# Second block: where the gates, the branch outputs and the token products lie in PSUM and in program order

## The chip, the cores and the metric

One core of one Trainium2 chip runs the whole program. The metric is the device time of one execution in microseconds. Its engines run side by side, each through its own queue in program order: TensorE (PE; its weight loads are listed as PEld), VectorE (DVE), ScalarE (ACT), GpSimd (POOL), and SyncE (SP), which issues the transfers.

## The reference, cut to what matters

Two transformer blocks follow one another on 256 tokens of width 1024. The change lies in the mixing half of the second:

```
z_a, q, k, v, gate_logits = split(h @ w_in)
u, v_ = split(gelu(z_a))
y_a = u * (tril(w_s) @ rms_norm(v_) + b_s)        # "token mixing", 768 wide
q, k = rope(q), rope(k)
y_b = dilated_mixture_attention(q, k, v)           # 256 wide
gates = sigmoid(gate_logits)                       # 2 x 1024 wide
merged = gates[0] * (y_a @ w_branch_a) + gates[1] * (y_b @ w_branch_b)
x = x + merged @ w_out
```

## The kernel before

Every weight matrix is cut into units of 128 x 1024 numbers, loaded in pairs through SyncE's queue. A unit is split into a high part `whi` (an ACT copy to the rounded type) and a low part `wlo` (a DVE subtraction), five units ahead of its use (`split_to(u + LA)` in `unit`). Activations are held in the same way, high and low: `xb` holds the normed input, transposed, as [feature, k, high|low, token], `xa` the output of the branches. A product is high x high + high x low + low x high. It is made in one of two forms:

- `mm3` (L223): three matmuls per k, each with its own weight load.
- `feature_unit` (L372): one matmul of 512 columns with `whi` against high and low joined, which lands in the two halves of a bank, and one of 256 columns with `wlo` into the first half. `join` (L382) then adds the halves: an ACT copy of the second, a DVE addition of the first. That addition frees the bank (`bank_free`).

Each engine's instructions are recorded in the order in which the Python code calls them, and each engine executes them in that order, stopping at the first whose semaphores aren't there. There is no planner: the order written by hand is the schedule. A `later(...)` function is run inside the next call of `unit`.

The order in the second block: `group_2` makes queries (groups 0 and 1, `qtok`), keys (2, 3, `ktok`), values (4, 5), and the second half of z_a (6, 7); a group of 512 columns has four units, one of 256 two. `rotate` applies the rotary embedding on POOL, `qk_transposes` (L1203) transposes two tiles of heads on TensorE and evicts them. After group 2's third unit (n == 2) stand two query transposes of two tiles each, after its fourth (n == 3) the third. Attention runs in four steps of `dl_scores`, `dl_probs` and `dl_out` between the units.

Then six `u_unit(c)` (banks c % 3) make u. `token_mix(i)` (L1307) is the product with w_s, 12, 8 and 12 matmul instructions for i = 0, 1, 2, in bank 4 + i; `token_gate(i)` (L1322) evicts it: two DVE operations into `yy`, a Gelu of u on ACT (`uT`), a DVE multiplication, an ACT copy and a DVE subtraction into `xa`. The last lines before the merge are L1378 to L1394.

The merge handles eight tiles d of 128 features. `merge_gate(d)` runs two feature units (gate of branch 0 and 1), joins them into `sg` and, in the next unit, applies the sigmoid (`squash`). `merge(d)` makes both branch outputs in bank 3, k 0 to 5 in columns 0:256, k 6 and 7 in columns 256:512, multiplies them with the gates (`mt`), adds the halves (`mx`) and splits the sum (`mh`, `ml`). The order of `merge_steps` is gate 0, gate 1, gate 2, branch 0, gate 3, branch 1, gate 4, and so on; from branch 4 on an output unit follows each branch unit, and four come at the end.

Of the kernel before, what the change touches and what calls it, by code (L numbers as in the profile page):

```python
# [7 lines left out]
ALU = mybir.AluOpType  # L8
# [6 lines left out]
KT = D // 128  # L15
# [143 lines left out]
def two_block_program(nc, T, out):  # L159
# [4 lines left out]
    def at(off, name, shape, dt=F32):  # L164
        return nc.alloc_sbuf_tensor_at(name, shape, dt, offset=off)
# [28 lines left out]
    xa = M("xa", [128, KT, 2, 256], F32R)  # L194
    xa_h, xa_l = xa[:, :, 0, :], xa[:, :, 1, :]
# [14 lines left out]
    pb = [nc.alloc_psum_tensor(f"bank{i}", [128, 512], F32) for i in range(8)]  # L210

    def semaphore(name):
        return nc.alloc_semaphore(f"s_{name}")

    sraw = [semaphore(f"raw{i}") for i in range(NR)]
    P, A, V, G = [Queue(semaphore(n)) for n in ("pe", "act", "dve", "pool")]
# [3 lines left out]
    def mm(o, l, r, start, stop, *w, inc=False):  # L220
        return P(lambda e: e.matmul(o, l, r, start=start, stop=stop), *w, inc=inc)  # L221

    def mm3(o, lh, ll, rh, rl, first, last, *w):  # L223

        mm(o, lh, rh, first, False, *w)
        mm(o, lh, rl, False, False)
        mm(o, ll, rh, False, last)

    def tr(o, i):
        P(lambda e: e.transpose(o, i, ident[:, :]), id_tok, inc=False)  # L230
# [4 lines left out]
    def copy(o, i, *w, **kw):  # L235
        return act(o, i, ACT.Copy, *w, **kw)

    def vcopy(o, i, *w):
        return V(lambda e: e.tensor_copy(o, i), *w)

    def tt(q, o, a, b, op, *w):
        return q(lambda e: e.tensor_tensor(out=o, in0=a, in1=b, op=op), *w)  # L242
# [32 lines left out]
    def flat(ap):  # L275
        return ap.rearrange("p a b -> p (a b)")
# [57 lines left out]
    def next_units(n):  # L334
        weights["unit"] += n
        return list(range(weights["unit"] - n, weights["unit"]))
# [3 lines left out]
    def later(fn):  # L340

        pending.append(fn)
# [17 lines left out]
    bank_free = {i: [] for i in range(8)}  # L360
# [11 lines left out]
    def feature_unit(u, bank, x, ready):  # L372

        h, l = unit(u)
        for k in range(KT):
            mm(pb[bank][:, :], h[:, k * 128:k * 128 + 128], flat(x[:, k, :, :]), k == 0, False,
               *(bank_free[bank] if k == 0 else []), *ready(k))
        for k in range(KT):
            mm(pb[bank][:, 0:256], l[:, k * 128:k * 128 + 128], x[:, k, 0, :], False, k == KT - 1)
        return release(u)  # L380

    def join(o, bank, p, *w):  # L382

        a = copy(o, pb[bank][:, 256:512], p, *w)
        v = tt(V, o, pb[bank][:, 0:256], o, ALU.add, a)
        bank_free[bank] = [v]
        return v
# [530 lines left out]
    def mix_1(k):  # L918
        return us[k], xb_h[:, k, :], xb_l[:, k, :], [ytok[k]]

    for k in range(KT - HOLD):
        u, lh, ll, w = mix_1(k)
        out_unit(u, (0, 1), lh, ll, k == 0, False, *w)
        release(u)
        if k == 0:
            ch_finish_0()
            P.wait(cv["out"], *bank_free[1])
            for t in range(2):
                for ft in range(2):
                    c = t * 256 + ft * 128  # L930
# [208 lines left out]
    qtok = at(xa_at, "qtok", [128, 2, 768])  # L1139
    ktok = at(xa_at + 6144, "ktok", [128, 2, 768])  # L1140
    N = Arena(C.lo)
    qt = N("qt", [128, 6, 256])
# [4 lines left out]
    sg = [K(f"sg{i}", [128, 512]) for i in range(4)]  # L1147
    mt = K("mt", [128, 512])
# [18 lines left out]
    def group_2(i, dst, c0, func=ACT.Copy):  # L1167

        w = GROUPS_2[i][1]
        banks = (2 * i % 3, (2 * i + 1) % 3)  # L1170
        us = next_units(w // 128)
        if i == 0:
            for n, u in enumerate(us):
                if n == 3:
                    norm_transposes(1, xb_h, xb_l)
                token_unit(u, (0,), xb_h, xb_l, banks, ready_x)
        for u in us:
            token_unit(u, (1,) if i == 0 else (0, 1), xb_h, xb_l, banks, ready_x)
            p = release(u)
            if u == us[-1]:  # L1180
                done[i] = []
                for t in range(2):
                    a = act(dst[:, t, c0:c0 + w], pb[banks[t]][:, 0:w], func, p)
                    bank_free[banks[t]] = [a]
                    done[i].append(a)
            yield

    def rotate(x, toks):

        r = []  # L1190
        for t in range(2):
            x3 = by64(x[:, t, :])
            x1, x2 = x3[:, :, 0:8], x3[:, :, 8:16]
            cos, sin = [rope[:, t, j, :].unsqueeze(1).broadcast_to([128, 12, 8]) for j in range(2)]
            m = [rtmp[:, j, :].rearrange("p (h d) -> p h d", d=8) for j in range(4)]
            for j, (a, b) in enumerate(((x1, cos), (x2, sin), (x1, sin), (x2, cos))):
                g = tt(G, m[j], a, b, ALU.mult, *toks, *rope_tok, *r)
            tt(G, x1, m[0], m[1], ALU.subtract, g)
            g = tt(G, x2, m[2], m[3], ALU.add)
            r = [g]  # L1200
        return r

    def qk_transposes(src, dst, b, bank, toks, scale):  # L1203
        P.wait(*toks, *bank_free[bank])
        for i in range(2):
            for t in range(2):
                tr(pb[bank][:, i * 256 + t * 128:i * 256 + t * 128 + 128], src[:, t, (b + i) * 128:(b + i) * 128 + 128])
        p = P.mark()
        if scale is not None:
            r = copy(flat(dst[:, b:b + 2, :]), pb[bank][:, :], p, scale=scale)  # L1210
        else:
            r = vcopy(flat(dst[:, b:b + 2, :]), pb[bank][:, :], p)
        bank_free[bank] = [r]
        return r
# [72 lines left out]
    def dl_finish():  # L1287
        o, src = xa_h[:, 6:8, :], pb[3][:, :].rearrange("p (k t) -> p k t", k=2)
        a = copy(o, src, *dl["out", 3])
        branch_tok.append(low(xa_l[:, 6:8, :], src, o, a))  # L1290
        bank_free[3] = [branch_tok[-1]]

    branch_tok = []
# [13 lines left out]
    def token_mix(i, toks):  # L1307

        bank = 4 + i
        P.wait(ws_tok, *toks, *bank_free[bank])  # L1310
        for c in (2 * i, 2 * i + 1):
            for t in range(2):
                o = (c % 2) * 256 + t * 128
                ga, gb = c * 128 // 192, (c * 128 + 64) // 192
                if ga == gb:
                    mm(pb[bank][:, o:o + 128], zv[:, t, c * 128:c * 128 + 128], ws[:, ga, :], True, True)
                else:
                    mm(pb[bank][0:64, o:o + 128], zv[:, t, c * 128:c * 128 + 64], ws[:, ga, :], True, True)
                    mm(pb[bank][64:128, o:o + 128], zv[:, t, c * 128 + 64:c * 128 + 128], ws[:, gb, :], True, True)
        mixed_tok[i] = P.mark()  # L1320
# [20 lines left out]
    def u_unit(c):  # L1341
        p = feature_unit(next_units(1)[0], c % 3, xb, lambda k: ready_x(k, 0) + ready_x(k, 1))
        u_tok[c // 2] = join(uT[:, c, :], c % 3, p, *junk_tok)
# [3 lines left out]
            pass  # L1347
    qr = rotate(qtok, done[0] + done[1])
    for n, _ in enumerate(group_2(2, ktok, 0)):
        if n == 2:  # L1350
            qT_tok = [qk_transposes(qtok, qt, 0, 4, qr, -0.125), qk_transposes(qtok, qt, 2, 5, qr, -0.125)]
        elif n == 3:
            qT_tok.append(qk_transposes(qtok, qt, 4, 6, qr, -0.125))
    for _ in group_2(3, ktok, 512):
        pass
    kr = rotate(ktok, done[2] + done[3])
# [20 lines left out]
    vn = v_norm()  # L1377
# [3 lines left out]
    u_unit(1)  # L1381
    u_unit(2)
    dl_probs(3)
    token_mix(0, vn)
    u_unit(3)
    dl_out(3)
    dl_finish()
    token_mix(1, vn)
    token_gate(0)
    u_unit(4)  # L1390
    token_mix(2, vn)
    u_unit(5)
    token_gate(1)
    token_gate(2)  # L1394
# [3 lines left out]
    sg_tok, m_tok, sum_tok = {}, {}, {}  # L1398

    def merge_gate(d):  # L1400
        for b, u in enumerate(next_units(2)):
            bank = (2 * d + b) % 3
            p = feature_unit(u, bank, xb, lambda k: [])
            v = join(sg[d % 4][:, 256 * b:256 * b + 256], bank, p, *sum_tok.get(d - 4, []))
        later(lambda: squash(d, v))
# [2 lines left out]
        sg_tok[d] = act(sg[d % 4][:, :], sg[d % 4][:, :], ACT.Sigmoid, v)  # L1408

    def merge(d):  # L1410
        bank, u = 3, next_units(1)[0]
        h, l = unit(u)
        P.wait(*branch_tok, *bank_free[bank])
        for k in range(KT):
            c = 0 if k < 6 else 256
            mm3(pb[bank][:, c:c + 256], h[:, k * 128:k * 128 + 128], l[:, k * 128:k * 128 + 128],
                xa_h[:, k, :], xa_l[:, k, :], k in (0, 6), k in (5, 7))
        p = release(u)
        v = tt(V, mt[:, :], pb[bank][:, :], sg[d % 4][:, :], ALU.mult, p, sg_tok[d])
        bank_free[bank] = [v]  # L1420
        x, h, l = mx[d % 2], mh[d % 6][:, :], ml[d % 6][:, :]
        v = tt(V, x[:, :], mt[:, 0:256], mt[:, 256:512], ALU.add, v)
        sum_tok[d] = [v]
        a = copy(h, x[:, :], v, *out_done.get(d - 6, []))
        m_tok[d] = low(l, x[:, :], h, a)

    out_done = {}
    for what, d in merge_steps():
# [4 lines left out]
        else:  # L1433
            u = next_units(1)[0]
# [10 lines left out]
    for t in range(2):  # L1445
        for hf in range(2):
            c = slice(hf * 512, hf * 512 + 512)
# [86 lines left out]
```

How the kernel before makes its waits and increments, by code:

```python
    def play(self, eng):  # L147
        for op in self.ops:
            if op[0] is None:
                eng.wait_ge(op[1], op[2])
            elif op[1] is True:
                op[0](eng).then_inc(self.sem, 1)
            elif op[1] is False:
                op[0](eng)
            else:
                op[0](eng).then_inc(op[1], 16)
```

## Time and profile before

| | |
|---|---|
| time, median of 3 | 699.97 us (699.76 to 700.63) |
| the profiled execution's own time | 699.81 us |
| its span, first to last instruction | 697.8 us |
| mean granted clock | 0.998 of full |
| PE busy / PE weight loads busy | 688.4 us (99%) / 593.5 us (85%) |
| DVE / ACT / POOL busy | 480.0 us (69%) / 405.5 us (58%) / 93.0 us (13%) |
| chain that ended last | PE 91%, POOL 2%, DVE 2%, ACT 2%, DMA 1% |

Shares of busy time are over the span; matmuls are pipelined, and a busy one contains its modelled drain, so a run of matmuls is to be read by the distance between starts. The gates, merges and output units of the second block lie between 415 and 499 us.

### The profile page before, as it was taken

Reading aid. Unit: us, or ns where it says so; the run is one execution under the profiler, and the core shown is the slowest. Engines: PE = TensorE matmul, PEld = TensorE weight load, DVE = VectorE, ACT = ScalarE, POOL = GpSimd, SP = SyncE. Lnnn points to the kernel's source line nnn. Section 1 sums busy time; section 2 is a strip of 40 time slices with the busy share of each in tenths; the row PEclk is TensorE's granted clock in tenths of the full one; section 3 lists DMA queues with packets and bytes.
Section 4 is the critical chain, followed back from the end, with each engine's and each line's share of the span. In section 5 each row is a group of like instructions: output and inputs, shape, how many; then the busy total and the mean of one; then the engine's idle time right before and its main releaser. Section 6 shows DMA issues by size and latency. Waiting matters only on the chain.

```text
span 697.8 us, 9554 instructions
## 1 busy us (share of the span) xinstructions
PE 688.4 (99%) x3880; PEld 593.5 (85%) x3880; DVE 480.0 (69%) x713; ACT 405.5 (58%) x678; POOL 93.0 (13%) x150
## 2 busy tenths in 40 slices
PE   9999999999999999999999999999999999999995
PEld 7888888888888888888888888999888888888884
DVE  5878687767666566667365767766668877777764
ACT  6776664656545455546545857554467665556552
POOL 2053022588200000002320000000000000000000
PEclk9999999999999999999999999999999999999999
DMA  8935533655555555536434334555454555555401
GB/s 318 393 138 178 222 127 136 243 187 198 198 204 185 185 188 204 201 128 218 175 125 178 121 122 181 187 188 200 150 189 173 197 219 188 181 185 185 173 1 60
DMA packets 20203, 126.13 MB, mean 181 GB/s; under 512 B 2496, under 2 KB 2752, under 8 KB 5952
## 3 DMA queue, kind: packets, MB, share of 16 engines
q1 hardware_dynamic: 19872, 125.01, 49.5%
q8 instruction: 30, 0.49, 0.3%
q10 hardware_dynamic: 288, 0.52, 0.3%
q14 instruction: 13, 0.11, 0.0%
HBM read 124.48 MB, written 1.05 MB: 180 GB/s over the span
## 4 chain that ended last, share of the span: by engine, by line
PE 91%; POOL 2%; DVE 2%; ACT 2%; DMA 1%; SPq 1%; issue 0%; POOLq 0%
PE bank L221 88%; PE bank L230 3%; POOL rtmp L242 1%; DMA raw<-in_w_dram 1%; ACT whi L233 1%; DVE wlo L242 1%; POOL ktok L242 0%; POOL qtok L242 0%; SPq L303 0%; SPq L490 0%; DVE sc L1238 0%; DVE xsq L242 0%; DVE yy L250 0%; DVE yy L242 0%; ACT L233 0%
## 5 line engine op out<-in xcount | busy, mean ns | idle before, releaser
L242 DVE TENSOR_TENSOR wlo<-raw,whi 128x1024 fp32r<-128x1024 f32 (+1 forms) x230 | 277.1, 1216 | 63.3 <-ACT whi L233 60.5
L233 ACT ACTIVATE whi<-raw 128x1024 fp32r<-128x1024 f32 (+1 forms) x230 | 235.3, 1036 | 3.5 <-PE bank L221 2.1
L221 PE MATMUL bank<-xb,whi 128*128 128x512 f32 x496 | 124.4, 393 | 0.3 <-DVE sg L242 0.2
L221 PE MATMUL bank<-xa,whi 128*128 128x512 f32 (+1 forms) x496 | 115.8, 365 | 0.0
L221 PEld LDWEIGHTS bank<-xb,whi 128*128 128x128 f32 x496 | 90.4, 188 | 18.1 <-DVE sg L242 0.4
L221 PEld LDWEIGHTS bank<-xa,whi 128*128 128x128 f32 x496 | 87.4, 189 | 13.7
L221 PE MATMUL bank<-whi,xb 128*128 128x512 f32 (+1 forms) x352 | 96.4, 355 | 0.0
L221 PEld LDWEIGHTS bank<-xb,wlo 128*128 128x128 f32 x496 | 67.6, 190 | 4.9
L221 PEld LDWEIGHTS bank<-whi,xb 128*128 128x128 f32 x352 | 62.1, 189 | 9.3 <-issue 0.3
L221 PE MATMUL bank<-xa,wlo 128*128 128x256 f32 x432 | 69.4, 282 | 0.0
L221 PE MATMUL bank<-xb,wlo 128*128 128x256 f32 x496 | 69.1, 282 | 0.0
L221 PEld LDWEIGHTS bank<-xa,wlo 128*128 128x128 f32 x432 | 62.5, 190 | 3.6
L221 PE MATMUL bank<-wlo,xb 128*128 128x512 f32 (+1 forms) x176 | 61.7, 351 | 0.0
L247 POOL TENSOR_SCALAR mean<-ss 128x1 f32<-128x1 f32 x8 | 2.4, 299 | 441.9 <-ACT xn L233 437.3
L221 PE MATMUL bank<-whi,xa 128*128 128x512 f32 (+1 forms) x192 | 56.5, 378 | 0.4 <-ACT whi L233 0.4
L221 PEld LDWEIGHTS bank<-whi,xa 128*128 128x128 f32 x192 | 34.8, 188 | 7.5 <-ACT whi L233 1.2
L221 PEld LDWEIGHTS bank<-wlo,xb 128*128 128x128 f32 x176 | 33.4, 190 | 4.0
L221 PE MATMUL bank<-whi,hhmix_norm_g 128*128 128x512 f32 x88 | 34.6, 393 | 0.0
L221 PE MATMUL bank<-whi,hhfinal_norm_g 128*128 128x512 f32 x88 | 34.5, 392 | 0.0
L221 PE MATMUL bank<-wlo,hhmix_norm_g 128*128 128x512 f32 x88 | 34.5, 392 | 0.0
L221 PE MATMUL bank<-wlo,hhfinal_norm_g 128*128 128x512 f32 x88 | 34.5, 392 | 0.0
L221 PE MATMUL bank<-wlo,xa 128*128 128x512 f32 (+1 forms) x96 | 34.4, 372 | 0.0
(228 smaller groups left out, 883.0 us busy)
## 6 DMA issues: line engine op xcount, KB each, us to landing
raw<-in_w_dram SPq DMA_DIRECT2D x109, 1024.0 KB, 4.8
raw<-in_w_dram SPq DMA_DIRECT2D x4, 512.0 KB, 8.6
raw<-in_w_dram SPq DMA_DIRECT2D x6, 256.0 KB, 7.0
bias<-in_bias_dram SPq DMA_DIRECT2D x1, 1024.0 KB, 9.0
xres<-in_x_dram SPq DMA_DIRECT2D x1, 1024.0 KB, 6.9
xt<-in_xt_dram SPq DMA_DIRECT2D x3, 264.0 KB, 6.7
raw<-in_w_dram ACTq DMA_DIRECT2D x2, 256.0 KB, 5.0
gain<-in_ffn_norm_w_dram SPq DMA_DIRECT2D x1, 512.0 KB, 8.5
```

The costliest lines, as they stand in the source:

```text
L221: return P(lambda e: e.matmul(o, l, r, start=start, stop=stop), *w, inc=inc)
L230: P(lambda e: e.transpose(o, i, ident[:, :]), id_tok, inc=False)
L233: return A(lambda e: e.activation(o, i, f, **kw), *w)
L242: return q(lambda e: e.tensor_tensor(out=o, in0=a, in1=b, op=op), *w)
L247: return q(lambda e: e.tensor_scalar(o, a, s1, s2, op0=op0, op1=op1), *w)
```

## The change

Four edits. The three pairs of query transposes come together after group 2's last unit. The three token products come together after `dl_finish`, and the first token gate moves behind `u_unit(4)`. The gates alternate between two banks in place of three. The branch outputs take the form of `feature_unit`, with branch a in bank 2 and branch b in bank 3, each joined by `join` into a half of `mt`, which is then multiplied with the gates in SBUF.

```
     for n, _ in enumerate(group_2(2, ktok, 0)):
-        if n == 2:
-            qT_tok = [qk_transposes(qtok, qt, 0, 4, qr, -0.125), qk_transposes(qtok, qt, 2, 5, qr, -0.125)]
-        elif n == 3:
-            qT_tok.append(qk_transposes(qtok, qt, 4, 6, qr, -0.125))
+        if n == 3:
+            qT_tok = [qk_transposes(qtok, qt, 2 * i, 4 + i, qr, -0.125) for i in range(3)]
...
     dl_probs(3)
-    token_mix(0, vn)
     u_unit(3)
     dl_out(3)
     dl_finish()
-    token_mix(1, vn)
+    for i in range(3):
+        token_mix(i, vn)
+    u_unit(4)
     token_gate(0)
-    u_unit(4)
-    token_mix(2, vn)
     u_unit(5)
     token_gate(1)
     token_gate(2)
...
     def merge_gate(d):
         for b, u in enumerate(next_units(2)):
-            bank = (2 * d + b) % 3
+            bank = b
...
     def merge(d):
-        bank, u = 3, next_units(1)[0]
+        u = next_units(1)[0]
         h, l = unit(u)
-        P.wait(*branch_tok, *bank_free[bank])
+        P.wait(*branch_tok)
         for k in range(KT):
-            c = 0 if k < 6 else 256
-            mm3(pb[bank][:, c:c + 256], h[:, k * 128:k * 128 + 128], l[:, k * 128:k * 128 + 128],
-                xa_h[:, k, :], xa_l[:, k, :], k in (0, 6), k in (5, 7))
+            bank = 2 + k // 6
+            mm(pb[bank][:, :], h[:, k * 128:k * 128 + 128], flat(xa[:, k, :, :]), k in (0, 6), False,
+               *(bank_free[bank] if k in (0, 6) else []))
+        for k in range(KT):
+            mm(pb[2 + k // 6][:, 0:256], l[:, k * 128:k * 128 + 128], xa[:, k, 0, :], False, k in (5, 7))
         p = release(u)
-        v = tt(V, mt[:, :], pb[bank][:, :], sg[d % 4][:, :], ALU.mult, p, sg_tok[d])
-        bank_free[bank] = [v]
+        for b in range(2):
+            v = join(mt[:, 256 * b:256 * b + 256], 2 + b, p, *sum_tok.get(d - 1, []))
+        v = tt(V, mt[:, :], mt[:, :], sg[d % 4][:, :], ALU.mult, v, sg_tok[d])
```

## Rows read from the trace of the kernel before

**Rows 1.** The page's head and the clock row of its 40 slices.

```profile
span 697.8 us, 9554 instructions
...
PEclk9999999999999999999999999999999999999999
```

**Rows 2.** The page's chain that ended last, by engine.

```profile
PE 91%; POOL 2%; DVE 2%; ACT 2%; DMA 1%; SPq 1%; issue 0%; POOLq 0%
```

**Rows 3.** Timeline around the query transposes: start, us, engine, operation, [idle before <-releaser].

```profile
334.45 0.39 PE L221 MATMUL bank<-whi,xb 128*128 128x512 f32 x1
334.98 0.86 PEld L230 LDWEIGHTS bank<-ident,qtok 128*128 128x128 f32 x8 [0.57 <-POOL qtok L242]
...
335.83 0.48 PE L221 MATMUL bank<-whi,xb 128*128 128x512 f32 x1
...
338.44 0.40 PE L221 MATMUL bank<-whi,xb 128*128 128x512 f32 x1
...
338.67 0.60 PE L230 MATMUL bank<-ident,qtok 128*128 128x128 f32 x4
...
339.03 0.36 PE L221 MATMUL bank<-whi,xb 128*128 128x256 f32 x1
```

**Rows 4.** Timeline of PE from the last attention step to the gate units.

```profile
401.29 0.82 PE L230 MATMUL bank<-ident,sc 128*128 128x128 f32 x6
402.36 1.30 PE L221 MATMUL bank<-ws,zv 128*128 128x128 f32 x12 [0.25 <-ACT pt L233]
...
415.21 2.00 PE L221 MATMUL bank<-xb,whi 128*128 128x512 f32 x8
...
420.79 2.00 PE L221 MATMUL bank<-xb,whi 128*128 128x512 f32 x8
...
423.93 2.14 PE L221 MATMUL bank<-xb,whi 128*128 128x512 f32 x8 [0.18 <-DVE sg L242]
...
426.84 2.00 PE L221 MATMUL bank<-xb,whi 128*128 128x512 f32 x8
```

**Rows 5.** Timeline of PE: first matmuls of branch unit 0 and of the gate behind it.

```profile
432.43 0.40 PE L221 MATMUL bank<-xa,whi 128*128 128x256 f32 x2
...
435.31 2.00 PE L221 MATMUL bank<-xb,whi 128*128 128x512 f32 x8
```

**Rows 6.** Busy time by engine in one period: PE, PEld, DVE, ACT, POOL, clock, DMA.

```profile
432.30:440.80 8.50, 8.50 (x59) 7.83 (x58) 6.20 (x9) 4.55 (x7) 0.00 (x0) 1.00 0.63 237
```

**Rows 7.** Timeline of ACT in u units 4, 5 and the token gates.

```profile
408.11 1.28 ACT L233 ACT_TABLE_LOAD   x1
409.41 0.63 ACT L233 ACTIVATE uT<-uT 128x512 f32<-128x512 f32 x1
410.87 0.63 ACT L233 ACTIVATE xa<-yy 128x512 fp32r<-128x512 f32 x1 [0.83 <-DVE yy L242]
...
412.35 0.37 ACT L233 ACTIVATE uT<-bank 128x256 f32<-128x256 f32 x1
...
415.41 0.38 ACT L233 ACTIVATE uT<-bank 128x256 f32<-128x256 f32 x1 [1.74 <-PE bank L221]
```

**Rows 8.** Timeline of DVE: additions for u units 4, 5 and gate unit 0.0.

```profile
413.62 0.42 DVE L242 TENSOR_TENSOR uT<-bank,uT 128x256 f32<-128x256 f32 x1
...
415.82 0.42 DVE L242 TENSOR_TENSOR uT<-bank,uT 128x256 f32<-128x256 f32 x1 [0.65 <-ACT uT L233]
...
423.46 0.42 DVE L242 TENSOR_TENSOR sg<-bank,sg 128x256 f32<-128x256 f32 x1
```

**Rows 9.** Timeline of PE: the last matmul of the program.

```profile
690.45 0.39 PE L221 MATMUL bank<-whi,hlfinal_norm_g 128*128 128x512 f32 x1
```

**Rows 10.** Windows after the last matmul, columns as in rows 6.

```profile
695.00:696.00 1.00, 0.00 (x0) 0.00 (x0) 0.00 (x0) 0.00 (x0) 0.00 (x0) 0.54 1.07 369
```

**Rows 11.** Timeline of the program's start: the first matmuls' weight loads.

```profile
1.09 4.34 PEld L221 LDWEIGHTS bank<-ones 128*128 128x128 f32 x20 [1.09 <-POOL ones L266]
```

## The prediction

> **What bounds the kernel now.** I first read the head of the page and its slices [rows 1], to see whether the end is set by one engine and whether TensorE's clock ever moves: the slice row shows the granted clock full in all forty slices. Then the chain that ended last [rows 2]: 91% of it is TensorE, POOL, DVE and ACT have 2% each. So the kernel is a nearly unbroken stream of matmuls, and an edit counts only if it changes the spacing of matmuls or makes TensorE wait. That sends me to the timelines around the four edited places, in order of time: query transposes [rows 3], token mixing and first gates [rows 4], merge [rows 5, 6]. There I read the start of each matmul group, not its busy time: the ends are modelled and overlap.
>
> **Query transposes.** The last matmul of unit 2 starts at 334.45, the first transpose at 334.98 [rows 3]. The ordinary distance is 0.23 (338.44 to 338.67, where nothing is waited for), so some 0.30 us of this 0.53 is the wait for POOL's rotation that the weight-load row names. One unit (2.8 us) later the rotation is long done and the wait goes. The twelve transposes are the same: 8 took 0.85 and 4 took 0.36 to the next matmul [rows 3]; at the first rate 12 take 1.28, against 1.21. Net -0.3 + 0.07, minus about 0.07 for the restart after them that unit 3 no longer pays: **-0.3 us** (bounds -0.2 to -0.4). The three ACT evictions that now stand together delay weight splits by about half a microsecond, of units needed five units later: nothing. The key transposes wait for their own rotation as before.
>
> **Token mixing.** Six transposes start at 401.29 [rows 4]; at 0.106 each (from the 8) they end at 401.93, and the first mixing product starts at 402.36: 0.43 us of waiting for ACT's copy of the probabilities. With unit 3 put there instead it goes. The products themselves are the same (all three mixings), they only lie together, and about 0.1 us of restart is saved at each of three joints with 512-column units that no longer follow a mixing product or a narrow tile. From 402.36 to the first gate matmul at 415.21 is 12.85 us; I take 12.57. First gate matmul after the change: 401.93 + 12.57 = **414.50**, -0.7 us; u unit 5 starts a unit earlier, at 414.50 - 2.79 = 411.7 (two gate units took 5.58, 415.21 to 420.79 [rows 4]).
>
> **Merge.** Before, 24 matmuls of 256 columns: 432.43 to 435.31, 2.88 us, 120 ns each [rows 5]. After, 8 of 512 and 8 of 256, which is the form of a gate unit: 2.79 to 2.80. The columns are the same; eight weight loads less. **-0.64 us** for eight merges (bounds 0 to -0.9). New beside it, per merge: two ACT copies of 128x256 (0.37 [rows 7]) and two DVE additions (0.42 [rows 8]). DVE is busy 6.20 and ACT 4.55 us in a period of 8.5 [rows 6]; they become 7.0 and 5.3, under 8.5. The merge's product comes about 1.2 us later, and is wanted only four merges later. Cost 0; if all of this were exposed, 8 x 1.25 = 10 us.
>
> **Two banks for the gates.** This is the term that decides. Units 0.0, 0.1, 1.0, 1.1 (gate.branch) used banks 0, 1, 2, 0; now 0, 1, 0, 1. The join of gate 0.0, which frees bank 0, is an ACT copy and a DVE addition. Both engines run in program order, and ahead of this join stand the token gates. Before, the addition began at 423.46 [rows 8], though its matmuls had ended about 418.0; gate 1.1 needed the bank, would have started at 420.79 + 2.79 = 423.58 and started at 423.93 [rows 4]: 0.35 us of waiting. After, gate 1.0 needs it, at 414.50 + 5.58 = **420.08**.
>
> And the join comes later than before, since token gate 0, formerly ahead of u unit 4, now follows it, and all three token gates are in front of gate 0.0's join. Step by step, spacings from [rows 7, 8]:
> - u unit 4 ends at 411.7; ACT copies it 0.20 after the next start (415.21 to 415.41), 411.91; the copy takes 0.38, so 412.30.
> - Now the table load for Gelu, 1.28 (it stood in a lull at 408.11): the Gelu starts at 413.60.
> - Gelu start to the copy into xa: 409.41 to 410.87, 1.46: 415.06. From there past a weight split to a u unit's copy, as 410.87 to 412.35: 1.48, 416.54.
> - DVE: from that copy to the unit's addition, behind the split's subtraction, as 412.35 to 413.62: 1.27, 417.8. Before, the addition for u unit 5 began at 415.82.
> - From there the two remaining token gates and the split are the same sequence as before: addition at 415.82 to the freed matmul at 423.93, 8.11 us. So bank 0 is there at **425.9**.
>
> TensorE waits from 420.08 to 425.9, **5.8 us**, where it waited 0.35. At the next units: gate 1.1 (bank 1) at +2.91 (423.93 to 426.84, the length after a wait) = 428.8; its bank's join ends about 427.3, no wait; gate 2.0 at 431.6, join of 1.0 ends about 429.8, no wait; then each gate bank has three units between uses. Gate 2.0 started at 426.84: **+4.75 us**, which holds the -0.7 and the old 0.35 already. What waits behind on TensorE is everything; no other work is put in this hole. Bounds: without the extra chain of token gate 0 (join as at 423.88) +2.7; with another 0.5 us on each of three token gates +6.2.
>
> The Trainium skill, "ScalarE: Activation LUTs", section "What ACT_TABLE_LOAD costs", adds a drain of about 1.38 us to every change of tables. In [rows 7] the Gelu starts at once after the load (408.11 + 1.28, then 409.41), so the trace does not show it in this place; by the page the hole would be 1.4 us longer, and I keep the trace's.
>
> **The clock.** A hole of nearly 6 us is longer than what the end of this trace shows to be enough: the last matmul starts at 690.45 and ends at 690.84 [rows 9], and in the stretch 695 to 696 the mean granted clock is 0.54 [rows 10], so it fell from 2.4 to 1.2 GHz right after 695.0, 4.2 us after the last work. In the new hole it would then fall before 425.9. What it costs to get it back, from the start [rows 11]: twenty 128-column matmuls load their weights in 4.34 us, 217 ns each, where transposes of that size run at 106 ns [rows 3]; the engine works some 4.3 us at half pace. Loss: 4.34 x (1 - 0.106/0.217) = 2.2; for 512 columns, spaced by 0.23 at the full clock, a little less. I take **+2.0 us** (0 to 2.7).
>
> The Trainium skill, "TensorE: Matmul & The Clock Gate", section "Why this matters for your kernels", warns of such pauses between bursts of matmuls, after which the engine is back at half its clock. That speaks against this change as the rows do.
>
> **Sum** against the profiled execution's 699.81 (0.16 under the median of 699.97): -0.3 (query) + 4.75 (mixing, gates) - 0.64 (merge) + 2.0 (clock) = +5.8: **705.6 us**.
>
> **Rivals.**
> 1. The hole, but the clock stays up through it. The fall was seen once, 4.2 us after the last work, and may come at other delays; a hole of 5.6 us after the last matmul's end need not hold it. 705.6 - 2.0 = 703.6.
> 2. The other sign: the bank is free in time. Mechanism: the join of gate 0.0 is done by 420.1, so two banks are enough, and only the gains are left: gate 2.0 at 414.50 + 4 x 2.79 = 425.66, -1.2, with -0.3 and -0.64: 697.7. Against it: that join began at 423.46 even before the change. It decides only if token gates took under half of their rows.
> 3. A shorter hole, 2 to 3 us: token gate 0 gets done inside u unit 4's time, join as before at 423.9. Then +2.7 - 0.3 - 0.64 without a fall of the clock: 701.6. Against it: the Gelu stands behind u unit 4's copy in program order, and with it the table load.
> 4. The merge stage chokes: the longer chain copy, copy, add, add, multiply, add keeps ACT and DVE from the weight splits, and TensorE waits for weights in each merge. 1.25 us exposed in a half of them adds 5: 710. Against it: 1.5 us of DVE's period are left and weights are split five units ahead.
>
> **How the numbers follow.** Forecast 0.50, rival 1 0.32, rival 2 0.04, rival 3 0.08, rival 4 0.06. The forecast's own range is 704.4 to 707.4 (clock loss 0.8 to 2.7, hole half a microsecond longer or shorter). From rival 1's lower side to that upper end, 702.8 to 707.4, is 0.8 of it. A measurement tells 0.2% (1.4 us) from no change. Faster by more than that is rival 2 alone, 0.04; within it, parts of rivals 2 and 3, 0.04; slower 0.92.
>
> **What would show it.** In the profile after: TensorE idle once for 5 to 6 us, released by the DVE addition into sg, at the third gate unit; the clock row below 1 in the slices around 60% of the span and matmuls of 512 columns spaced over 0.4 us for some microseconds; the table load for Gelu behind u unit 4's copy; no wait for qtok at the transposes, none for pt after the probabilities; merges 0.08 us shorter. The prediction is wrong if the gate join does not stand behind all three token gates, if the chain of a token gate shrinks when it has other neighbours, or if splits come late in the merge.

## The result and the profile after

The changed kernel takes 705.73 us (median of 6, 704.89 to 706.17), the kernel before 699.96 in the same rounds: ratio 1.0076, 95% interval 1.0063 to 1.0089. The forecast was 705.6, in a range of 702.8 to 707.4. Its profiled execution took 705.88 us.

The head of the page, busy time by engine, and the clock row of its slices, which answer to [rows 1]:

```profile
span 704.0 us, 9455 instructions
PE 688.6 (98%) x3816; PEld 591.6 (84%) x3816; DVE 485.3 (69%) x729; ACT 410.8 (58%) x694; POOL 94.4 (13%) x150
PEclk9999999999999999999999998999999999999998
```

The span is 6.2 us longer, and PE's busy time has hardly moved (688.4 to 688.6): the time lost is mostly time in which TensorE stands still. The clock row has two 8s: one in the slice from 422 to 440 us, and one in the last slice, where it falls at 700.5, behind the last matmul. Who made TensorE's weight loads wait between 320 and 500 us (total, times, longest), after:

```profile
PEld bank L221 <- DVE sg L242: 5.9, 1, 5.9
PEld bank L221 <- issue: 2.4, 10, 0.4
PEld bank L230 <- POOL ktok L242: 0.6, 1, 0.6
```

The waits for qtok and for pt, which [rows 3] and [rows 4] show, are gone; the wait for sg was 0.4 and is 5.9. The query transposes, in the timeline of PE:

```profile
337.29 0.39 PE L221 MATMUL bank<-whi,xb 128*128 128x512 f32 x1
337.52 1.47 PE L230 MATMUL bank<-ident,qtok 128*128 128x128 f32 x12
338.75 0.36 PE L221 MATMUL bank<-whi,xb 128*128 128x256 f32 x1
```

They follow the unit at the ordinary 0.23, take 1.23 for all twelve, and group 3 starts at 338.75, where it started at 339.03. Next the same engine from the last attention step to gate 2.0, against [rows 4]:

```profile
400.99 0.82 PE L230 MATMUL bank<-ident,sc 128*128 128x128 f32 x6
401.57 2.09 PE L221 MATMUL bank<-xb,whi 128*128 128x512 f32 x8
...
405.35 3.62 PE L221 MATMUL bank<-ws,zv 128*128 128x128 f32 x32
408.72 2.09 PE L221 MATMUL bank<-xb,whi 128*128 128x512 f32 x8
...
411.60 2.00 PE L221 MATMUL bank<-xb,whi 128*128 128x512 f32 x8
...
414.39 2.00 PE L221 MATMUL bank<-xb,whi 128*128 128x512 f32 x8
...
417.19 2.00 PE L221 MATMUL bank<-xb,whi 128*128 128x512 f32 x8
...
425.79 3.78 PE L221 MATMUL bank<-xb,whi 128*128 128x512 f32 x8 [5.65 <-DVE sg L242]
429.37 1.77 PE L221 MATMUL bank<-xb,wlo 128*128 128x256 f32 x8
430.98 2.00 PE L221 MATMUL bank<-xb,whi 128*128 128x512 f32 x8
...
433.77 2.00 PE L221 MATMUL bank<-xb,whi 128*128 128x512 f32 x8
```

Gate 0.0 starts at 414.39 (0.8 earlier), gate 0.1 at 417.19, and gate 1.0, due 2.79 later at 419.98, starts at 425.79: 5.81 us late. It then takes 5.19 us to the next unit. Why it waits is in the timelines of ACT and DVE, in program order, beside [rows 7, 8]:

```profile
411.80 0.38 ACT L233 ACTIVATE uT<-bank 128x256 f32<-128x256 f32 x1 [4.79 <-PE bank L221]
412.20 1.28 ACT L233 ACT_TABLE_LOAD   x1
413.50 0.63 ACT L233 ACTIVATE uT<-uT 128x512 f32<-128x512 f32 x1
414.96 0.63 ACT L233 ACTIVATE xa<-yy 128x512 fp32r<-128x512 f32 x1 [0.83 <-DVE yy L242]
...
416.44 0.36 ACT L233 ACTIVATE uT<-bank 128x256 f32<-128x256 f32 x1
```

```profile
414.23 0.69 DVE L242 TENSOR_TENSOR yy<-yy,uT 128x512 f32<-128x512 f32 x1 [0.81 <-ACT uT L233]
...
417.71 0.42 DVE L242 TENSOR_TENSOR uT<-bank,uT 128x256 f32<-128x256 f32 x1
...
425.32 0.42 DVE L242 TENSOR_TENSOR sg<-bank,sg 128x256 f32<-128x256 f32 x1
```

ACT waits 4.79 us for u unit 4, and only then come the table load, token gate 0, u unit 5's join (417.71, against 415.82 before), two more token gates, and at 425.32 the addition that frees bank 0, whose matmuls had ended near 417.4. The windows show the clock (columns as in [rows 6]):

```profile
423.00:424.00 1.00, 0.00 (x0) 0.00 (x0) 0.69 (x1) 1.00 (x2) 0.00 (x0) 1.00 0.00 0
424.00:425.00 1.00, 0.00 (x0) 0.00 (x0) 0.82 (x1) 1.00 (x3) 0.00 (x0) 0.51 0.00 0
...
430.00:431.00 1.00, 1.00 (x8) 1.00 (x7) 0.00 (x0) 0.00 (x0) 0.00 (x0) 0.58 0.81 303
431.00:432.00 1.00, 1.00 (x7) 0.82 (x6) 0.41 (x1) 0.82 (x2) 0.00 (x0) 1.00 1.05 442
```

It fell to 1.2 GHz at 424.0, 3.9 us after the last matmul's end, and was back at 2.4 GHz at 430.8: 6.8 us low, 5.05 of them with TensorE at work. All six executions have mean clocks of 0.992 to 0.994, those of the kernel before in the later rounds 0.996 to 0.999.

### The profile page after: what moved, and what is told of

The parts are those of the page before. It is cut to its first block, busy times and chain, and to the rows that moved or that the text cites. A ratio compares the mean times of both kernels' runs of the same rounds, so it can differ in the third digit from the quotient of the medians.

```text
span 704.0 us, 9455 instructions
## 1 busy us (share of the span) xinstructions
PE 688.6 (98%) x3816; PEld 591.6 (84%) x3816; DVE 485.3 (69%) x729; ACT 410.8 (58%) x694; POOL 94.4 (13%) x150
## 3 DMA queue, kind: packets, MB, share of 16 engines
HBM read 124.48 MB, written 1.05 MB: 178 GB/s over the span
## 4 chain that ended last, share of the span: by engine, by line
PE 92%; DVE 3%; ACT 2%; POOL 1%; DMA 1%; issue 0%; POOLq 0%; ACTq 0%; DVEq 0%
PE bank L221 89%; PE bank L230 3%; DMA raw<-in_w_dram 1%; ACT whi L233 1%; DVE wlo L242 1%; DVE wk L250 1%; POOL rtmp L242 1%; ACT wk L233 1%; POOL ktok L242 0%; ACT L233 0%; DVE sc L1238 0%; DVE yy L242 0%; ACT xa L233 0%; DVE yy L250 0%; DVE hst L253 0%
## 5 line engine op out<-in xcount | busy, mean ns | idle before, releaser
L221 PE MATMUL bank<-xb,whi 128*128 128x512 f32 x496 | 125.9, 396 | 5.8 <-DVE sg L242 5.7
L221 PE MATMUL bank<-xa,whi 128*128 128x512 f32 x432 | 108.3, 393 | 0.0
L221 PEld LDWEIGHTS bank<-xa,whi 128*128 128x128 f32 x432 | 78.9, 188 | 15.7
L221 PEld LDWEIGHTS bank<-xa,wlo 128*128 128x128 f32 x432 | 58.9, 190 | 4.2
L221 PE MATMUL bank<-xa,wlo 128*128 128x256 f32 x432 | 60.2, 282 | 0.0
L233 ACT ACTIVATE gamix_norm_g<-bank 128x256 f32<-128x256 f32 x22 | 8.4, 380 | 44.6 <-PE bank L221 44.6
```

The source lines that it names most:

```text
L233: return A(lambda e: e.activation(o, i, f, **kw), *w)
```

## The experiments

Two groups: each edit by itself on the kernel before, then repairs of the changed kernel. All were timed in five rounds beside the kernel before, whose medians were 699.98 (first four) and 699.81 us (the others). Places in two traces are compared by distances inside each trace, because the same code lies up to half a microsecond earlier or later from one execution to the next (group 3 begins at 339.03 in one trace of unchanged code and at 339.55 in another).

**Query transposes alone.**

```
-        if n == 2:
...
-        elif n == 3:
...
+        if n == 3:
+            qT_tok = [qk_transposes(qtok, qt, 2 * i, 4 + i, qr, -0.125) for i in range(3)]
```

> The kernel before with the query transposes moved alone. Theory of the prediction: the wait for POOL's rotation goes, 0.3 us faster (ratio 0.9996), and the traced span is 697.5. Rival, that the evictions standing together delay the weight splits: no gain, or slower by up to 0.5 us.

699.26 us, ratio 0.9992 (0.9984 to 1.0001). The interval takes in both the expected 0.3 us and nothing; the time cannot show it, the trace can: from the transposes of the normed input ahead of group 0 to the start of group 3 it is 25.88 us (312.63 to 338.51), before 26.27 (312.76 to 339.03), a gain of 0.39.

**Joined branch outputs alone.**

```
     def merge(d):
-        bank, u = 3, next_units(1)[0]
...
-            mm3(pb[bank][:, c:c + 256], h[:, k * 128:k * 128 + 128], l[:, k * 128:k * 128 + 128],
...
+            bank = 2 + k // 6
+            mm(pb[bank][:, :], h[:, k * 128:k * 128 + 128], flat(xa[:, k, :, :]), k in (0, 6), False,
...
+            v = join(mt[:, 256 * b:256 * b + 256], 2 + b, p, *sum_tok.get(d - 1, []))
```

> The kernel before with the joined branch outputs in banks 2 and 3 alone; the gates still use banks 0 to 2, so a gate unit can meet a branch bank. Theory of the prediction: 2.80 in place of 2.88 us for each of eight branch units, 0.6 us faster (ratio 0.9991), unless a gate unit waits for bank 2. Rival, that the longer chain on ACT and DVE is exposed: slower by 1 to 10 us, with waits of TensorE for wlo in the merge.

702.83 us, ratio 1.0043 (1.0030 to 1.0056): slower by 2.9 us. No wait is for wlo; the waits for weight loads between 320 and 500 us that are new are for banks:

```profile
PEld bank L221 <- DVE sg L242: 3.0, 3, 1.5
...
PEld bank L221 <- DVE mt L242: 1.1, 1, 1.1
```

One of the three waits for sg is the 0.4 us of before; the others and the one for mt are new, 3.7 us in all, and less the 0.7 gained in eight merges they are the 3 us. So this edit needs the one beside it: while gates go round banks 0, 1, 2, a branch unit in bank 2 follows directly on a gate unit in it, and the other way round. The exception in the expectation decided, not the rival. In the changed kernel, with gates in 0 and 1, these waits don't occur.

**Two banks for the gates alone.**

```
-            bank = (2 * d + b) % 3
+            bank = b
```

> The kernel before with the gates in two banks alone, token gate 0 still ahead of u unit 4. Program-order theory: gate 1.0 waits from 420.79 to about 423.9, 3.1 us in place of 0.35, slower by 2.8 us (ratio 1.0040) with the clock up. Rival, that two banks by themselves make the whole hole of 5.7 us: slower by 5 us or more, with the clock's fall 7.

703.76 us, ratio 1.0051 (1.0039 to 1.0063), +3.8. Timeline of PE, and windows:

```profile
424.23 2.56 PE L221 MATMUL bank<-xb,whi 128*128 128x512 f32 x8 [2.96 <-DVE sg L242]
426.59 1.91 PE L221 MATMUL bank<-xb,wlo 128*128 128x256 f32 x8
428.30 2.38 PE L221 MATMUL bank<-xb,whi 128*128 128x512 f32 x8
...
431.47 2.00 PE L221 MATMUL bank<-xb,whi 128*128 128x512 f32 x8
```

```profile
424.00:425.00 1.00, 0.77 (x3) 0.67 (x4) 1.00 (x2) 1.00 (x2) 0.00 (x0) 1.00 0.57 66
425.00:426.00 1.00, 1.00 (x5) 0.82 (x4) 1.00 (x3) 0.98 (x2) 0.00 (x0) 0.84 0.42 164
426.00:427.00 1.00, 1.00 (x4) 0.81 (x4) 0.77 (x1) 0.95 (x2) 0.00 (x0) 0.50 0.98 418
```

The hole is the expected 3 us, not the whole one. What was not expected is that the clock falls after it, at 425.7, when TensorE has been working again for 1.5 us. The two units then take 4.07 and 3.17 in place of 2.91 and 2.79: 1.5 us lost. The clock isn't the whole spread of the five times: the two executions without a fall by their mean clock (0.999) took 702.60 and 703.76.

**The order alone**: token products together, token gate 0 behind u unit 4.

```
+    for i in range(3):
+        token_mix(i, vn)
+    u_unit(4)
     token_gate(0)
-    u_unit(4)
```

> The kernel before with the token products together and token gate 0 behind u unit 4 alone, gates still in three banks. Program-order theory: the join of gate 0.0 comes at 425.8 in place of 423.9, and gate 1.1 waits for it some 3 us from 422.9 on, slower by 1.9 us (ratio 1.0027). Rival, that the order is harmless and only the number of banks counts: the wait of 0.4 us before the token products goes, 0.5 to 0.7 us faster.

703.27 us, ratio 1.0042 (1.0028 to 1.0057), +3.3. Gate 1.1 waits, as expected:

```profile
425.50 2.11 PE L221 MATMUL bank<-xb,whi 128*128 128x512 f32 x8 [2.87 <-DVE sg L242]
```

The profiled execution took 701.3 us at a mean clock of 0.999, which is near the expected +1.9; the other five took 701.87 to 704.58 at 0.996 to 0.998. The median is above the expectation, and the interval (2.0 to 4.0 us) just leaves it out; that the clock makes the difference fits these means, but no trace of a slower execution was kept. Each of the two edits alone makes a hole of 3 us; together they make one of 5.8.

**Token products together, token gate 0 left ahead of u unit 4**, three banks.

> The kernel before with the three token products put together behind the last attention step, token gate 0 still ahead of u unit 4, gates in three banks, merge and query transposes as before. Theory of the prediction: the wait for the probabilities' copy goes (0.43) and some restarts, gate 0.0 starts 0.7 us earlier, the wait of gate 1.1 stays near 0.3: 0.7 us faster (ratio 0.9990). Rival, that the token gates' chain is fixed by other things (the products' end now later in the queue): gate 1.1 waits 0.7 us longer and nothing is gained.

699.52 us, ratio 0.9995 (0.9986 to 1.0004): within what can be told from nothing. In the trace gate 0.0 starts 13.40 us after the attention's transposes, before 13.92 (401.29 to 415.21): 0.5 us, not 0.7. Gate 1.1 still waits 0.18, as before, so the gain isn't eaten there, as the rival had it.

**The changed kernel with token gate 0 ahead of u unit 4.**

```
     for i in range(3):
         token_mix(i, vn)
-    u_unit(4)
     token_gate(0)
+    u_unit(4)
```

> The changed kernel with token gate 0 put back ahead of u unit 4. Program-order theory: its chain runs during u unit 4, the join of gate 0.0 ends near 423.1, the hole shrinks from 5.7 to about 3.1 us; against the kernel before +2.1 us (ratio 1.003) with the clock up, +4 if the clock falls in a hole of this length too. Rival, that the two banks alone make the hole: as the changed kernel, +6.

701.94 us, ratio 1.0034 (1.0020 to 1.0048). Gate 1.0 in the timeline of PE:

```profile
422.81 2.53 PE L221 MATMUL bank<-xb,whi 128*128 128x512 f32 x8 [2.96 <-DVE sg L242]
```

The hole is 2.96 us, as expected, and in this trace too the clock fell only after it, at 424.3, and cost 1.5 us in two units. That the median is at the expected +2.1 is luck: with the clock up the changed kernel's +5.8, less 2.0 for the clock and 2.7 for the shorter hole, leaves +1.2, and the fall brings the rest. The twelve times lie from 700.41 to 704.69, and they go with the mean clock of the execution: 700.41, 700.49, 700.82 and 701.01 at 0.997; 704.58, 704.63 and 704.69 at 0.993.

**The hole filled**: twenty products of ones (128 columns) ahead of gate 1.0 in the changed kernel. Nothing is left out; the products go to a bank that nobody reads.

```
     def merge_gate(d):
+        if d == 1:
+            P.wait(*bank_free[7])
+            for _ in range(20):
+                mm(pb[7][:, 0:128], ones[:, :], ones[:, :], True, True)
+            bank_free[7] = [P.mark()]
```

> The changed kernel with twenty products of ones (128 columns, 40 matmul instructions, some 4.4 us) into bank 7 put into the hole ahead of gate 1.0. Clock theory: the granted clock stays full, gate unit 1.0 takes 2.9 in place of 5.2 us, and the time is 2.3 us under the changed kernel's, +3.7 against before (ratio 1.0053). Rival, that the long gate unit is a price of the wait itself and not of the clock: no difference, ratio 1.0083 or more.

703.63 us, ratio 1.0049 (1.0037 to 1.0061), 2.1 us under the changed kernel (1.95, if each is set against the kernel before of its own rounds), and the intervals of the two ratios don't meet. Timeline of PE:

```profile
420.40 4.63 PE L221 MATMUL bank<-ones 128*128 128x128 f32 x40
426.21 2.11 PE L221 MATMUL bank<-xb,whi 128*128 128x512 f32 x8 [1.19 <-DVE sg L242]
428.16 1.12 PE L221 MATMUL bank<-xb,wlo 128*128 128x256 f32 x8
429.11 2.00 PE L221 MATMUL bank<-xb,whi 128*128 128x512 f32 x8
```

The unit comes 5.81 us after its turn, as without the filling, but takes 2.90 in place of 5.19 us, with the clock full. So 2.3 us of the long unit are the clock, and the hole's 5.8 are the wait.

**The hole of 3 us filled**, ten products, in the kernel with token gate 0 first.

> The changed kernel with token gate 0 ahead of u unit 4 and ten products of ones (20 matmul instructions, 2.2 us) into bank 7 in the hole of 3.0 us ahead of gate 1.0. Clock theory: in some executions a hole of 3 us lets the clock fall and costs 1 to 4 us, in others not, which is why the times without the filling lie from 700.4 to 704.7; with it all lie within 1 us near 700.4 (ratio 1.0008 to 1.0012). Rival, that the spread is something else: it stays, and the median stays near 702.

700.91 us, ratio 1.0027 (1.0006 to 1.0047). Of eleven times ten lie from 700.22 to 701.99; one is 708.78 with a mean clock of 0.947, 5% under all others of this kernel, which a fall in one hole cannot give and which stays unexplained; the query transposes alone had one like it (701.47 us at 0.948), so it isn't this edit's. The ten lie over 1.8 us, more than the expected 1; the times near 704.6 don't occur. In the trace the filling leaves 0.73 us of idling, the clock stays up, and the unit takes 2.90. The median is +1.1, near the +1.2 that is left without the clock's fall. The two ratio intervals overlap, so this run supports the clock's part and doesn't prove it.

**The table for Gelu loaded early**, in the changed kernel.

```
+    A(lambda e: e.preload_act_table_set("gelu_and_others"), inc=False)
     u_unit(4)
     token_gate(0)
```

> The changed kernel with the table for Gelu loaded ahead of u unit 4's weight split, in a lull of ACT, in place of behind that unit's copy. If the load stands in the chain of token gate 0 as the rows say, the DVE multiplication starts when the two operations before it end, 0.8 us earlier, the hole is 4.9 in place of 5.65 us, and the time 0.8 us under the changed kernel's (ratio to before 1.0072). If a change of tables cost 1.4 us more than its load: 2.2 us under (ratio 1.005). Rival, that the load was hidden: no difference (1.0083).

704.57 us, ratio 1.0067 (1.0055 to 1.0080), 1.2 us under the changed kernel's median; the two intervals overlap, so the traces have to decide. Timelines of DVE and PE:

```profile
413.01 0.69 DVE L242 TENSOR_TENSOR yy<-yy,uT 128x512 f32<-128x512 f32 x1
```

```profile
424.58 3.78 PE L221 MATMUL bank<-xb,whi 128*128 128x512 f32 x8 [4.89 <-DVE sg L242]
```

The multiplication now starts with no wait for the Gelu, and the hole is 4.89 in place of 5.65: 0.76 of the load's 1.28 us stood in the chain, the rest lay under two DVE operations. The Trainium skill, "ScalarE: Activation LUTs", section "What ACT_TABLE_LOAD costs", puts a drain of 1.38 us on top of a change of tables; these rows have no room for it (load 412.20 + 1.28, Gelu at 413.50), and the hole shrank by what the load alone gives.

**A repair: gate 1 in banks 2 and 3**, which are empty until branch 0.

```
-            bank = b
+            bank = b + 2 * (d == 1)
```

> The changed kernel with gate 1's two units in banks 2 and 3 and all others in 0 and 1. Program-order theory: the first use of bank 0 again is gate 2.0, ready at 425.6, its bank at about 425.8: the hole all but goes, and with the other gains the time is 1.8 to 2.0 us under before (ratio 0.9973). Rival, that another wait takes its place (bank 2 still held by u unit 5, or the merge chain exposed): no faster than before.

697.93 us, ratio 0.9975 (0.9966 to 0.9985). Gate 2.0 is the first to ask for bank 0 again, and starts at

```profile
425.77 2.11 PE L221 MATMUL bank<-xb,whi 128*128 128x512 f32 x8
```

0.24 us after its turn. The late join is as late as it was (bank 0 free at the same 425.8); it only meets nobody.

**The same with token gate 0 first.**

> As the kernel with gate 1 in banks 2 and 3, and token gate 0 ahead of u unit 4 too. Program-order theory: bank 0 is free near 423, two microseconds before gate 2.0 asks, no wait at all: 2.0 to 2.2 us under before (ratio 0.997), at most 0.2 us better than with four banks alone. Rival, that token gate 0's place costs something else (its Gelu table ahead of u unit 4's split): 0.5 us slower than four banks alone.

697.64 us, ratio 0.9968 (0.9956 to 0.9980), the fastest of all; no wait for sg is left. It beats the kernel before by 2.2 us.

**That kernel with the merge of before.**

> The kernel with gate 1 in banks 2 and 3 and token gate 0 first, with the merge of before (three matmuls of 256 columns, bank 3). If the joined form is worth its 0.08 us a merge and its ACT and DVE work is hidden, this is 0.6 us slower than with it: 1.4 us under before (ratio 0.9980). Rival, that the longer chain eats the gain: no difference between the two.

698.08 us, ratio 0.9973 (0.9963 to 0.9983). The medians are 0.44 us apart, in the expected direction, and the intervals overlap, so the times don't settle it. The traces are plainer: from gate 0.0 to the first closing transposes it is 88.20 us with the old merge (414.36 to 502.56) and 87.47 with the joined one (413.91 to 501.38).

## Why the prediction was right

**Query, -0.3:** 339.03 became 338.75, but this execution was 0.09 us later up to group 0 (312.85 in place of 312.76), so the edit itself is worth 0.37 (25.90 in place of 26.27 us), inside the bounds.

**Mixing, -0.7:** measured -0.52 (13.40 in place of 13.92 us). The wait of 0.43 went as forecast; the restarts did not give the other 0.28: the three products take 3.37 us together (405.35 to 408.72), where apart they took 3.20 (1.23, 0.92 and 1.05 to the matmul behind each). An error of 0.2 us.

**The chain to the freed bank:** forecast u unit 5's addition at 417.8 and the bank at 425.9; the trace has 417.71 and 425.79. Due time of gate 1.0: 420.08 and 419.98. Hole: 5.8 and 5.81. That the two edits alone each make 3 us, and that moving token gate 0 back or the gates to unused banks takes the hole in half or away, shows both parts of the mechanism: the join stands behind three token gates, and two banks ask for it one unit earlier than three.

**The clock, +2.0:** measured 5.19 - 2.91 = 2.28 in the trace, and 2.1 between the medians with the hole filled. The term came out to 0.3 us, in part by luck. The same twenty weight loads take 4.34 us in the trace before and 3.76 in the one after, so the scale itself moves from one execution to the next. And the granted clock reads 1.00 in every window of the program's first six microseconds, so that the clock made that start slow was an inference from the spacing; the hole filled supports it (forty such loads take 4.55 us at the full clock, 114 ns each, in place of 217). What was read too simply is the clock row of [rows 1]: a 9 means 90% or more, and its last slice holds the fall at 695. Rival 1 (the clock stays up) did not happen in the profiled execution, and the six times, 704.89 to 706.17 at mean clocks of 0.992 to 0.994, leave no room for one without a fall, which would be near 703.6 as with the hole filled (0.997 to 0.998). What I had wrong is which holes are in danger: rival 3 counted a hole of 2 to 3 us without a fall, and so did the expectations of two experiments. Two of the three traces with a hole of 3 us have one. Nor is the delay of 4.2 us a constant: from the end of the last matmul to the fall it was 3.1 us with the table loaded early, 3.9 in the changed kernel, 4.4 and 4.5 in the two with holes of 2.96. The Trainium skill, "TensorE: Matmul & The Clock Gate", section "Why this matters for your kernels", warns of pauses between bursts; the runs here side with its warning, since two holes of 2.96 us were followed by the lower clock.

**Merge, -0.64:** branch 0 to the closing transposes is 70.71 us (439.35 to 510.06), before 71.44 (432.43 to 503.87): -0.73. The first two rows are of the changed kernel, the last of the kernel before:

```profile
439.35 2.00 PE L221 MATMUL bank<-xa,whi 128*128 128x512 f32 x8
...
510.06 1.03 PE L230 MATMUL bank<-ident,xn 128*128 128x128 f32 x8
```

```profile
503.87 1.03 PE L230 MATMUL bank<-ident,xn 128*128 128x128 f32 x8
```

The ACT and DVE work beside it was hidden, rival 4 is out: DVE is busy 8.82 of 11.3 us in 466.1 to 477.4, and no wait for weights appears. Not foreseen in the prediction: this edit depends on the gates' staying out of bank 2, as the run with it alone shows.

**Sum:** -0.37 for the query transposes, +0.09 for the execution's later start of group 0, -0.52 for the mixing, 5.81 - 0.35 for the hole, 2.28 for the clock, -0.73 for the merge: +6.2, which is the difference of the spans (704.0 - 697.8). The medians differ by 5.77. The forecast was +5.8; against the trace it is 0.4 short, 0.3 of it the clock's price, 0.2 the mixing's gain and 0.1 the later start, less 0.1 each for the merge and the query transposes. So that the forecast meets the median to 0.1 us is luck; that it is right in its terms is not. The range was not worked out cleanly: the bounds in its brackets give 703.9 to 706.8 rather than 704.4 to 707.4, and the measured time lies in either.

## What to carry to other kernels

A buffer is not free when its matmuls end but when its eviction has had its turn: before taking away a buffer, walk the evicting engines' queues in program order from a point that both versions share, and compare the time found with the due time of the next user. Count a hole in TensorE's stream twice, as its length and as the half-speed stretch behind it; holes of 3 us already cost that in some executions here. And an edit whose gain rests on a free bank is measured with the edit that frees it.

## What the runs showed that I had not expected

- The clock can fall after a hole has ended: with a hole of 2.96 us it went down 1.5 us into the new work and cost 1.5 us there. With the other hole of 2.96 us it did the same, and with one of 2.87 us, in a third kernel, it stayed up.
- A hole of 3 us makes the time itself vary: 700.41 to 704.69 us over twelve executions of one program, in step with mean clocks of 0.997 to 0.993. So up to 4 us more or less with one and the same hole of 3. No trace of an execution near 704.6 was kept. Its mean clock is that of the changed kernel, where the low stretch lasted 6.8 us; all of it under work would lose 3.4 us, an estimate that would bring 701.0 to 704.4.
- Two edits that each cost 3 to 4 us (medians +3.8 and +3.3) cost 7.2 us together in the trace of the changed kernel (5.81 - 0.35 for the hole, 2.28 for the clock, less the mixing's 0.52). So here their prices added up. For the wait the traces show why: one edit lets a unit ask for the bank one unit earlier (3.13 us late alone), the other makes the same join come later (3.04 late alone), and once TensorE waits, both count in full: 3.13 + 3.04, less the old 0.35 once, is 5.82. That the clock's share adds up too is not shown.
